# Seven seams reordered, and two latent norms taken by quarters of the tokens

## The reference, cut to what matters

```python
# first block
x = layer_norm(ALPHA * x + 0.5 * swiglu(x, w1, w3, w2), ln1_g, ln1_b)
q_lat, kv_lat, k_rope, u, g_a, g_b = split(x @ w_in)      # 384, 256, 32, 512, 1024, 1024
y_a = mla_attention(rms_norm(q_lat), rms_norm(kv_lat), k_rope) @ w_o_attn
y_b = s5_branch(u) @ w_o_ssm                              # two state-space scans and a GLU
x = layer_norm(ALPHA * x + (sigmoid(g_a) * y_a + sigmoid(g_b) * y_b) @ w_out, ln2_g, ln2_b)
x = layer_norm(ALPHA * x + 0.5 * swiglu(x, ...), ln3_g, ln3_b)
x = layer_norm(ALPHA * x + sigmoid(x @ ple_w_gate) * (p @ ple_w_proj), ln4_g, ln4_b)
# second block
state = rglru(rms_norm(ctx) ... )                         # 256 context tokens
h = rms_norm(x) * (1 + scale) + shift
y = mix(h)        # eleven planes of h @ w_in; a 4-tap conv with a gated scan, a 3-tap conv,
                  # a gated 31-tap conv with a layer norm, box means; then @ w_out
out = rms_norm(x + gate * y, final_g)
```

## Time and profile before

| what | value |
|---|---|
| median of 3 runs | 3123.17 us (3119.57 to 3123.41) |
| time of the profiled execution | 3120.53 us |
| its span, first to last instruction | 3118.7 us |
| PE busy | 3075.9 us, 99% |
| PEld, DVE, ACT busy | 80%, 74%, 39% |
| mean granted TensorE clock | 0.997 of full |

### The profile page before, as it was taken

One profiled execution on the slowest core, in us unless ns is written; L12 is line 12 of the kernel. 1 busy time (PEld: TensorE's weight loads), 2 busy tenths in 40 slices (PEclk: granted clock), 3 DMA queues, 4 the chain that ended last, 5 costly groups with the idle time before them and its releaser, 6 DMA issues.

```text
span 3118.7 us, 38749 instructions
## 1 busy us (share of the span) xinstructions
PE 3075.9 (99%) x15342; PEld 2501.0 (80%) x15342; DVE 2316.6 (74%) x3975; ACT 1225.1 (39%) x1894; POOL 56.2 (2%) x49
## 2 busy tenths in 40 slices
PE   8999999999999999999999999999999999999998
PEld 6887888887988887777888888888877788788887
DVE  6777767777859678888578766766776789789636
ACT  4233323335242455554243232222365634534414
POOL 0000000000000001130000000000000000000000
PEclk9999999999999999999999999999999999999999
DMA  3222221223333351012212111111211321122242
GB/s 132 75 70 79 77 66 62 73 69 128 106 96 136 125 198 47 8 55 108 108 42 68 41 54 61 48 54 48 68 62 46 115 77 64 48 70 102 81 169 75
DMA packets 89252, 250.21 MB, mean 80 GB/s; under 512 B 8560, under 2 KB 24816, under 8 KB 87536
## 3 DMA queue, kind: packets, MB, share of 16 engines
q1 hardware_dynamic: 89072, 247.73, 23.5%
HBM read 203.65 MB, written 44.04 MB: 79 GB/s over the span
## 4 chain that ended last, share of the span: by engine, by line
PE 92%; DVE 5%; ACT 2%; DMA 1%; issue 0%; SPq 0%; DVEq 0%; ACTq 0%
PE PS L580 90%; PE PS L585 2%; DVE WS L2306 1%; DVE COLB L3113 0%; DMA RAW<-in_W 0%; DVE TMP L2306 0%; DVE X L2314 0%; ACT WS L1405 0%; ACT X L1405 0%; DVE TMP L2310 0%; DVE PT L3131 0%; DVE XC L2314 0%; ACT XS L1405 0%; DVE XS L2314 0%; ACT TMP L1405 0%
## 5 line engine op out<-in xcount | busy, mean ns | idle before, releaser
L580 PE MATMUL PS<-XS,WS 128*128 128x512 f32 (+1 forms) x6480 | 1511.1, 390 | 14.6 <-DVE XS L2306 9.2
L580 PEld LDWEIGHTS PS<-XS,WS 128*128 128x128 f32 x6480 | 1209.0, 188 | 285.4 <-issue 23.4
L580 PE MATMUL PS<-HS,WS 128*128 128x512 f32 x2208 | 510.4, 390 | 3.1 <-DVE TMP L2306 2.7
L580 PEld LDWEIGHTS PS<-HS,WS 128*128 128x128 f32 x2208 | 413.6, 188 | 92.0 <-DVE TMP L2306 3.5
L2306 DVE TENSOR_TENSOR WS<-RAW,WS 128x512 fp32r<-128x512 f32 (+1 forms) x398 | 347.4, 881 | 176.7 <-ACT WS L1405 176.1
L1405 ACT ACTIVATE WS<-RAW 128x512 fp32r<-128x512 f32 (+1 forms) x398 | 307.7, 779 | 401.9 <-PE PS L580 351.4
L2306 DVE TENSOR_TENSOR X<-PS,X 128x512 f32<-128x512 f32 x272 | 184.3, 689 | 102.3 <-PE PS L580 102.2
L2306 DVE TENSOR_TENSOR TMP<-TMP,PS 128x512 f32<-128x512 f32 x304 | 203.8, 683 | 69.5 <-PE PS L580 65.6
L580 PE MATMUL PS<-T,WS 128*128 128x512 f32 x960 | 230.6, 389 | 0.0
L580 PEld LDWEIGHTS PS<-T,WS 128*128 128x128 f32 x960 | 180.2, 188 | 37.4
L1405 ACT ACTIVATE TMP<-PS 128x512 f32<-128x512 f32 x144 | 85.2, 596 | 292.8 <-PE PS L580 276.3
(11 more groups left out here) (343 smaller groups left out, 3536.4 us busy)
## 6 DMA issues: line engine op xcount, KB each, us to landing
RAW<-in_W SPq DMA_DIRECT2D x263, 512.0 KB, 3.5
RAWX<-in_W SPq DMA_DIRECT2D x30, 512.0 KB, 3.5
DC<-TMP SPq DMA_DIRECT2D x32, 256.0 KB, 2.1
X<-in_xT SPq DMA_DIRECT2D x8, 512.0 KB, 8.9
DX<-X SPq DMA_DIRECT2D x2, 2048.0 KB, 8.4
DCZ<-CA SPq DMA_DIRECT2D x8, 512.0 KB, 4.3
DGA<-TMP SPq DMA_DIRECT2D x16, 256.0 KB, 2.2
DGB<-TMP SPq DMA_DIRECT2D x16, 256.0 KB, 2.9
```

Source lines behind the costliest of these rows:

```text
L580: done = d.matmul(out, l, r, start=first, stop=last)
```

## The change

Seven places are reordered and the latents' norms take another form:
1. `latents`: the first two output tiles of the first token half are computed together, tile k by tile k; the hooked mean product stands before k = 7 of the pair.
2. `latents` and `u_rows`: the latents' squares are summed in four column groups, root and reciprocal run on 128 columns in place, and products spread the result in the bank from which VectorE then scales. The sums move one tile later and the spreads stand later in the order.
3. `sync`: `loads(129)` moves ahead of the wait for the GLU and of the gate rows and two latents.
4. `embed`: the first two gate tiles are computed as a pair, with the hook before k = 6; their two embedding tiles follow.
5. `factor_slot("h", h)` goes ahead of `biased(h)` for both halves, and one hook in `first_planes` moves from k = 4 to k = 2.
6. `mixer` on VectorE: for the first channel tile, `UU` is computed between the two convolutions, and the release of two weight units comes after both.
7. The last two parts of the output norm are summed, rooted and inverted on 64 columns and spread by products.

```diff
+        def latent_sum(name, h, n):
+            use = ("sq", name, h)
+            banks.take(use, (ve, "lat", name, n - 1, h))
+            e.wait_ge(ve("ones"), *banks.free(use))
+            for k in range(n):
+                e.wait_ge(ac("sq", name, h, k))
+                src = tmp("sq", name, h, k)
+                mms([(bank(*use)[32 * g:32 * g + 32, 0:128], ones[:, 0:32], src[:, 128 * g:128 * g + 128], k == 0, k == n - 1)
+                     for g in range(4)]).then_inc(*mm.inc("sq", name, h, k))
+        def latent_spread(name, h):
+            e.wait_ge(ve("rs", name, h), dma("const")("cols"))
+            mms([(bank("sq", name, h)[:, 128 * g:128 * g + 128], ident[:, 32 * g:32 * g + 1].to_broadcast([128, 128]),
+                  tmp("rs", name, h)[:, 0:128], True, True) for g in range(4)]).then_inc(*mm.inc("rb", name, h))
 # tensor, latents()
-                if n == 5:
...
+                if n in (0, 5):
+                    i2, use2 = LATENTS[n + 1][0], ("lat", *LATENTS[n + 1])
...
+                        if (n, k) == (0, 7):
+                            hook()
...
-                        if (n, k) in ((1, 6), (2, 4), (3, 4), (4, 0)):
+                        if (n, k) in ((2, 4), (3, 4), (4, 0)):
...
-                if n in (6, 7):
-                    square_sum("kv", n - 6, 2, lambda k: tmp("sq", "kv", n - 6, k))
+                if n in (7, 8):
+                    latent_sum("kv", n - 7, 2)
                 if n == 10:
-                    square_sum("q", 0, 3, lambda k: tmp("sq", "q", 0, k))
+                    latent_spread("kv", 0)
+                    latent_spread("kv", 1)
+                    latent_sum("q", 0, 3)
 # tensor, u_rows()
                     if p == 0 and j == 0:
-                        square_sum("q", 1, 3, lambda k: tmp("sq", "q", 1, k))
+                        latent_spread("q", 0)
+                        latent_sum("q", 1, 3)
+                    if p == 0 and j == 2:
+                        latent_spread("q", 1)
 # tensor, embed()
+                if n == 0:
+                    pair = [("pg", *EMBED[j]) for j in range(2)]
...
+                    for k in range(8):
+                        if k == 6:
+                            hook()
...
 # tensor, first_planes()
-                        if h == 0 and (i, k) in ((0, 6), (1, 4), (2, 4), (4, 4)):
+                        if h == 0 and (i, k) in ((0, 6), (1, 4), (2, 4), (4, 2)):
 # tensor, outputs()
+            spread_out(1)
             row_squares(2)
+            spread_out(2)
 # scalar, embed() and mixer(); for h = 1 in the same way
             gate(11)
+            factor_slot("h", 0)
             biased(0)
-            factor_slot("h", 0)
             spread_copy("h", 0)
 # vector, latents()
             release(us[2])
-            normal("kv", 1, 2, 0)
             release(us[0])
-            normal("kv", 1, 2, 1)
+            for h in range(2):
+                rstd_rows("kv", h)
             pump(40)
             release(us[3])
-            normal("q", 3, 3, 0)
+            for h in range(2):
+                normal("kv", 1, 2, h)
+            rstd_rows("q", 0)
             release(us[4])
             release(us[5])
+            pump(8)
+            rstd_rows("q", 1)
+            normal("q", 3, 3, 0)
+            pump(20)
             normal("q", 3, 3, 1)
 # vector, mixer()
-                release(*us[:3 if ct else 2])
-                for h in range(2):
...
+                    if n == (1 if ct else 0):
+                        if ct:
+                            release(*us[:3])
+                        for h in range(2):
+                            e.wait_ge(ac("cg", ct, h), mm("ca", ct, h), ve("cv", ct - 1) if ct else ve("pad", "uu"))
+                            tt(UU[:, 15 + 512 * h:527 + 512 * h], tmp("cg", ct, h), bank("ca", ct, h), ALU.mult).then_inc(
+                                *ve.inc("uu", ct, h))
+                if ct == 0:
+                    release(*us[:2])
 # vector, outputs(): scale_out reads the factor from PSUM for p > 0
+                x, r = X[:, a:b, out_part(p)], bank("sq", "out", p)[:, 0:256] if p else held_part(p)
+                e.wait_ge(mm("rb", "out", p) if p else ve("rs", "out", p), ac("fg", b - 1, 1 if a > 3 and p else p))
 # sync
         for i in (1, 2, 3):
             load_latent(i)
+        loads(129)
         e.wait_ge(mm("glu", 3, 1))
         load_gate(0)
         load_gate(1)
         e.wait_ge(ve("glm", 3, 1))
         for i in (4, 5):
             load_latent(i)
-        loads(129)
```

More of the change, by code:

```diff
@@ L1175, in embed @@
                     side = norm_h(0)
-                banks.take(use, (ac, *use))
-                product8(us[m], h, use, "ln3", beside=True,
-                         within={1: (4,), 2: (4,), 3: (4,), 4: (0,), 8: (4,), 9: (4,), 10: (4,), 11: (4,), 12: (4,), 13: (0,)}.get(n))
+                if n == 0:
+                    pair = [("pg", *EMBED[j]) for j in range(2)]
+                    for j, other in enumerate(pair):
+                        banks.take(other, (ac, *other))
+                        e.wait_ge(w_hi(first[j]), w_lo(first[j]), *banks.free(other))
+                    for k in range(8):
+                        if k == 6:
+                            hook()
+                        e.wait_ge(ac("xs", "ln3", k, 0), ve("xs", "ln3", k, 0))
+                        for j, other in enumerate(pair):
+                            done = mms(group3(bank(*other), [(blk(first[j], 128 * k), xs_pair(k, 0))], first=k == 0, last=k == 7))
+                            if k == 7:
+                                done.then_inc(*mm.inc(*other))
+                elif n > 1:
+                    banks.take(use, (ac, *use))
+                    product8(us[m], h, use, "ln3", beside=True,
+                         within={2: (4,), 3: (4,), 4: (0,), 8: (4,), 9: (4,), 10: (4,), 11: (4,), 12: (4,), 13: (0,)}.get(n))
                 if h == 1 or m < 4:
@@ L1364, in outputs, with spread_out @@
                         row_squares(1)
+            spread_out(1)
             row_squares(2)
+            spread_out(2)
         def row_squares(p):
             use = ("sq", "out", p)
[L1370 to L1376, removed]
+            e.wait_ge(ve("sqs", 6 if p else 7, p))
+            if p == 0:
+                banks.take(use, (ac, "rs", "out", p))
+                e.wait_ge(*banks.free(use))
+                done = mms([(bank(*use), ones[:], held_part(p), True, True)])
+            else:
+                banks.take(use, (ve, "fin", p, 3))
+                e.wait_ge(*banks.free(use))
+                for i, src in enumerate((held_part(p), tmp("sq", "out", p, 3))):
+                    if i:
+                        e.wait_ge(ac("sq", "out", p, 3))
+                    done = mms([(bank(*use)[32 * g:32 * g + 32, 0:64], ones[:, 0:32], src[:, 64 * g:64 * g + 64], i == 0, i == 1)
+                                for g in range(4)])
             done.then_inc(*mm.inc("sq", "out", p, 7))
+        def spread_out(p):
+            e.wait_ge(ve("rs", "out", p), dma("const")("cols"))
+            mms([(bank("sq", "out", p)[:, 64 * g:64 * g + 64], ident[:, 32 * g:32 * g + 1].to_broadcast([128, 128]),
+                  tmp("rs", "out", p)[:, 0:64], True, True) for g in range(4)]).then_inc(*mm.inc("rb", "out", p))
         ffn("ln1", "x", True)
@@ L1450, in root @@
             use = ("rs", name, h)
-            tmps.take(use, (ve, *(end or use)))
+            tmps.take(use, (mm, "rb", name, h) if width < 256 else (ve, *(end or use)))
             e.wait_ge(var, ve("eps"), *tmps.free(use))
@@ L2252, in square @@
                 if p == 2 and m == 1:
-                    root("out", 1, 1024, RMS_EPS, mm("sq", "out", 1, 7), width=256)
+                    root("out", 1, 1024, RMS_EPS, mm("sq", "out", 1, 7), width=64)
                 e.wait_ge(ac(*use))
@@ L2271, in outputs @@
                     square(m, p, *((ve, "sqs", 4 + m, p) if m < 3 else (mm, "sq", "out", p, 7)))
-            root("out", 2, 1024, RMS_EPS, mm("sq", "out", 2, 7), width=256)
+            root("out", 2, 1024, RMS_EPS, mm("sq", "out", 2, 7), width=64)
         for h in range(2):
```

34 lines of the change are left out of this document (15 added, 19 removed).

## The result

The changed kernel takes 3131.05 us (median of 9 runs, 3129.02 to 3132.68) against 3123.07 us of the kernel before on the same chip (9 runs, 3119.57 to 3123.56). The ratio is 1.0029, 95% interval 1.0019 to 1.0039: slower by 8 us, where 3122.7 and a range up to 3129 had been forecast. The profiled execution has a span of 3128.6 us, 9.9 more than before.

The account below looks back on a forecast made before the run. TensorE is busy 3075.9 of 3118.7 us, so only its 43 us of standing and lowered clock can be won. Eight terms sum to −0.5, taking 3123.17 to 3122.7 us; 8-in-10 range 3114.5 to 3129.

Parts of the forecast that it names:

- UU: UU between the mixer's convolutions: its bank is freed earlier, −1.1 us, range −1.1 to +1.0.
- term 3: loads(129) ahead of the context's gate rows: +3.3 us, range −4.0 to +5.0.
- Context: Moved loads: near 0 from a new 4 us wait for VectorE's low half; +3.3 us from later gate rows.
- Embedding: Embedding's first pair: wait of 3.4 to 3.9 us and lowered clock, +2.7 us, range +1.0 to +3.5.
- h, both halves: Root ahead of the additions: first half −4.6 us, second half +1.3 us from a later copy of the spread.
- term 5: Root first, first half of h: spread earlier, clock kept, next mean waits 1.4 to 1.5; net −4.6 us.
- Norms and output: Latents' norms by quarter sums and spreads: −3.1 us; output norm with shorter reciprocal but added spread: about +0.4 us.
- Rival B: Joined waits across latents, context, embedding and h lower the clock, 1.5 us being enough: 3130.5 us; chance 0.17.
- the latents: Latents' first pair: short waits become one of 2.0 to 2.4 us, at the clock's edge, +0.6 us.

Follow-up runs that it names:

- e2: Changed kernel with the release of the first two weight units ahead of UU instead of behind both convolutions: 3125.71 us, ratio 1.0014.
- e6: Changed kernel with the GLU wait and the first two gate-row loads ahead of loads(129): 3125.14 us, ratio 1.0012.
- e5: Changed kernel with loads(129) put back behind the gate rows and latents: 3125.2 us, ratio 1.0012.
- e7: e6 with VectorE releasing the context's second raw unit ahead of its two convolutions: 3124.17 us, ratio 1.0012.
- e13: e8 with SP's and VectorE's order in the context as in the kernel before: 3113.47 us, ratio 0.9975.
- e14: Changed kernel with loads(129) and the embedding's pair as before, UU's second half behind both convolutions: 3116.44 us, ratio 0.9981.
- e8: Changed kernel with e7's context, UU's second half behind both convolutions, both pairs and h's second-half root order as before: 3114.94 us, ratio 0.9979.
- e9: e8 with VectorE's first four gate-row products in the context ahead of the last three low halves: 3116.77 us, ratio 0.9986.
- e3: Changed kernel with only UU's first half between the convolutions, the releases ahead of its second half: 3125.5 us, ratio 1.0015.
- e1: Changed kernel with UU put back as before: 3127.42 us, ratio 1.0018.
- e12: Changed kernel with the hook of the embedding's pair at k = 7 instead of k = 6: 3130.45 us, ratio 1.0028.
- e11: Kernel before with only h's first-half root ahead of the additions and the hook at k = 2: 3118.09 us, ratio 0.9986.
- e10: Kernel before with only the latents' norms by quarters: 3116.25 us, ratio 0.9985.

## Why the prediction was wrong

**UU, the step that failed.** The prediction said that the wait for UU's second product "holds VectorE for some 5 us until it comes, which VectorE has as slack here". The 5 us were right (5.29), the wait of 0.98 did go, and VectorE had that slack for its own rows. What was missed is who else waits for VectorE there: in the new order the releases of two weight units stand behind the wait and the second convolution. The prediction put no cost on them, though its own term 3 has loads that wait for raw slots freed by VectorE. e2 shows it: with the releases ahead, VectorE stands 3.02 us until the same product, and TensorE loses nothing. The term was −1.1 and measured +5.1.

**Context.** Both waits came, and for the reasons given: about 4 us for VectorE's low half (4.05), and one behind the late gate rows. The size was off by 4.4 us. VectorE's products with GBR start 5.1 us later than before (1141.91 for 1136.79), not 3.1: they ran 1141.91 − 1135.08 = 6.8 us after the issue of the gate rows, not 3.8. That TensorE's second wait is 3.14, as the 3.1 of the sum, is luck, since TensorE itself arrives 1.5 us later than before. The other part is the clock, which cost 5.1 us in the stage where before it cost about 0.03 x 60 = 1.8: I had let it fall once, as before, and it fell behind both waits. e6 shows that SP's queue order alone makes the 6.4 us between the changed kernel and e5.

**VectorE and the context's limit.** That loading earlier does not bring TensorE further is shown: e5, e6 and e7 end the stage at +1.3, +1.3 and +1.4 with the loss at three different places. TensorE's waits in the stage are 3.7, 4.0 and 3.6 us there, and 3.7 in e13 with the loads as before. What is left between these stages (0.0 in e13 and e14, +1.3, +2.5 in e8) goes with how long the half clock behind the waits lasts. That VectorE's unbroken work is the limit (theory V) is not shown: in e9 its products came 2.7 us earlier than in e8 and ScalarE's copy took the place. As I read the rows, the stage has a loop (low half, raw slot, load, high half) on which both depend.

**Embedding.** Direction and wait were right (3.82 in the 3.4 to 3.9); the half clock lasted longer than taken. It varies: with a wait of 3.8 us the stage costs 3.0 in e3, e5 and e6, near the 2.7 of the sum, and 3.9 to 4.1 in the changed kernel, e1, e2 and e7. e12 has the shorter wait and the shorter half clock together, 1.6.

**h, both halves.** −5.1 for −4.6, as the next mean waited 0.67 and not 1.5; e11 has it alone. +1.1 for +1.3: the copy out of the spread came late, as forecast, and TensorE waited 1.54 us for what follows from it instead of 0.38. The hook that moved to k = 2 was read wrongly: the prediction set it beside the mean of its term 5, but it is the spread of the second half. 12 products stand ahead of that spread before (the step from 2420.00 to 2423.01) and 6 after. With the root first no wait stands there; without it 1.35 us, and the stage costs 0.7 (e8, e9, e11, e13). The best kernel, e13, still has it; putting it back there is untried.

**Norms and output.** −2.15 for −3.1. The wait of 0.86 went, and no new idle over 0.1 us came. But the products were priced by their records, which overlap what comes next: counted from the start of one group to the start of the product behind it, the ten by `ones` took 7.1 us and not 8.6, so the exchange of products saved 0.7 and not 2.1; the wait and the short steps around it gave the rest. e10 has the norms alone. Output: −0.1 for +0.4. From the start of the last sums to the last scaling it is 4.10 us, and 4.05 before: the spread came, but the sums, which the term left out, also got shorter (0.44 for 1.12).

**Clock.** Rival B (joined waits lower the clock) was half right: it did so in the context and the embedding, not at the latents or h = 0, and not at 1.5 us. Its 3130.5 lies close to the measured 3131.05, but by luck: of its 7.8 us the latents, h = 0 and the second half of h did not come, and the 6.2 us of UU are not in it. The rule of the Trainium skill cited (TensorE: Matmul & The Clock Gate, section HAM oscillation — how this bites in real kernels) is contradicted here for an idle of 2.0 us, behind which the clock is 0.57. For the latents' wait of 2.45 us it came out right in this profile, and not in six of the ten that have that wait.

## What to carry to other kernels

Before a wait is put into an engine's order, list what that engine hands out behind it (freed slots, halves, releases), and follow each to the loads and the other engines; slack on the engine's own rows says nothing about them. On one queue in program order, a small load that someone needs soon should stand ahead of a batch whose last members wait for free slots. And where three engines feed each other through slots, taking away one wait moves it: look for where the same microseconds stand in the next trace before the edit is counted as a gain.

## What the runs showed of the hardware

The same wait does not always lower the clock. The idle of 2.00 to 2.03 us at 65 us stands in all 16 profiles; behind it is a stretch of half clock in 12 of them and none in 4 (the kernel before among these). Behind the latents' idle of 2.43 to 2.46 us there is one in 6 of 10 profiles, behind the embedding's of 3.79 to 3.82 in 7 of 7, behind the idle of 1.40 to 1.44 us of h = 0 in none of 14. So an edit next to such a wait can gain or lose 1.7 us far from its place, and a single profile doesn't tell.

How long a load takes hung on what was issued around it. The DMA issues of the changed kernel between 1134 and 1137 us (KB each, median us from issue to landing), for the last row:

```profile
GBR<-DGB SPq DMA_DIRECT2D x2, 512.0 KB, 7.1
LR<-DL SPq DMA_DIRECT2D x2, 512.0 KB, 8.8
RAW<-in_W SPq DMA_DIRECT2D x1, 512.0 KB, 4.6
```

The same two gate-row loads took 3.8 us before, when nothing else was issued within 4 us of them. Here a weight load of the same size was issued 0.4 us ahead of them and two latent rows within 1.4 us behind.
